# Four different row lengths for the tensors that the weight products stream from

## What is computed

```
swiglu(h):   (silu(h @ w_gate) * (h @ w_up)) @ w_down
conv_ffn(h): u = conv3(h @ w_up) + b;  (silu(u[:F]) * u[F:]) @ w_down
x = x + 0.5 * swiglu(norm(x)); x = x + token_mixing(norm(x))
x = x + cross_attention(norm(x), norm(mem)); x = x + 0.5 * swiglu(norm(x))
h = [meta; norm(x)]
for i in 0, 1: h = h + norm(mixer_i(norm(h))); h = h + norm(conv_ffn_i(norm(h)))
```

## Time and profile before

| | |
|---|---|
| median of 3 runs | 2238.99 us (2238.66 to 2241.04) |
| the profiled execution | span 2237.2 us from the first to the last instruction; 1.8 us less than the median of the runs |
| PE busy | 2184.0 us (98%), 14,619 products |
| DVE, ACT, POOL busy | 1354.7 us (61%), 999.2 us (45%), 960.0 us (43%) |
| mean granted clock of TensorE | 0.994 |
| DMA | 194.40 MB, mean 87 GB/s |

### The profile page before, as it was taken

One profiled execution on the slowest core, in us unless ns is written; L12 is line 12 of the kernel. 1 busy time (PEld: TensorE's weight loads), 2 busy tenths in 40 slices (PEclk: granted clock), 3 DMA queues, 4 the chain that ended last, 5 costly groups with the idle time before them and its releaser, 6 DMA issues.

```text
span 2237.2 us, 37596 instructions
## 1 busy us (share of the span) xinstructions
PE 2184.0 (98%) x14619; PEld 1971.6 (88%) x14619; DVE 1354.7 (61%) x2104; ACT 999.2 (45%) x1950; POOL 960.0 (43%) x709
## 2 busy tenths in 40 slices
PE   8999999999999999999999999999999979999998
PEld 6799998888887788989897779999999969989897
DVE  5785765637634557848577665762635797536255
ACT  4454453432443434636454446442423554424234
POOL 3644435642472455444451115244444503544443
PEclk9999999999999999999999999999999989999999
DMA  5243333331351223333310113133233301233331
GB/s 163 78 121 97 99 108 97 85 88 48 101 160 57 85 76 110 111 91 114 95 57 27 35 39 105 39 93 96 85 95 90 100 29 57 94 104 94 94 89 72
DMA packets 336251, 194.40 MB, mean 87 GB/s; under 512 B 7357, under 2 KB 327506, under 8 KB 336098
## 3 DMA queue, kind: packets, MB, share of 16 engines
q1 hardware_dynamic: 335570, 191.13, 29.2%
q10 hardware_dynamic: 528, 1.19, 0.2%
HBM read 190.20 MB, written 2.10 MB: 86 GB/s over the span
## 4 chain that ended last, share of the span: by engine, by line
PE 82%; DVE 11%; ACT 3%; issue 2%; POOL 1%; DVEq 0%; DMA 0%; POOLq 0%; ACTq 0%; SPq 0%
PE PS L830 17%; PE PS L834 17%; PE PS L832 17%; PE PS L1202 5%; PE PS L1203 5%; PE PS L1204 5%; PE PS L1125 2%; PE PS L1123 2%; PE PS L1124 2%; PE PS L3025 1%; PE PS L3008 1%; PE PS L3052 1%; PE PS L3070 1%; DVE u_conv L1651 1%; DVE mst L3258 1%
## 5 line engine op out<-in xcount | busy, mean ns | idle before, releaser
L754 POOL TENSOR_TENSOR w_lo<-raw,w_hi 128x512 fp32r<-128x512 f32 (+3 forms) x549 | 748.9, 1387 | 956.8 <-ACT w_hi L770 956.4
L770 ACT ACTIVATE w_hi<-raw 128x512 fp32r<-128x512 f32 (+3 forms) x549 | 305.0, 604 | 466.6 <-PE PS L834 362.5
L830 PE MATMUL PS<-XHI,w_hi 128*128 128x264 f32 (+2 forms) x1736 | 421.9, 308 | 4.1 <-DVE XLO L919 3.9
L834 PE MATMUL PS<-XHI,w_lo 128*128 128x264 f32 (+2 forms) x1736 | 413.2, 303 | 0.0
L832 PE MATMUL PS<-XLO,w_hi 128*128 128x264 f32 (+2 forms) x1736 | 413.0, 303 | 0.0
L830 PEld LDWEIGHTS PS<-XHI,w_hi 128*128 128x128 f32 x1736 | 280.0, 189 | 23.4 <-issue 6.5
L834 PEld LDWEIGHTS PS<-XHI,w_lo 128*128 128x128 f32 x1736 | 279.4, 189 | 13.4
L832 PEld LDWEIGHTS PS<-XLO,w_hi 128*128 128x128 f32 x1736 | 279.7, 189 | 13.1 <-issue 1.2
L830 PE MATMUL PS<-h_hi,w_hi 128*128 128x512 f32 (+2 forms) x588 | 180.1, 342 | 4.1 <-POOL w_lo L754 2.5
L832 PE MATMUL PS<-h_lo,w_hi 128*128 128x512 f32 (+2 forms) x588 | 179.5, 341 | 0.0
L834 PE MATMUL PS<-h_hi,w_lo 128*128 128x512 f32 (+2 forms) x588 | 179.5, 341 | 0.0
(11 more groups left out here) (567 smaller groups left out, 5420.9 us busy)
## 6 DMA issues: line engine op xcount, KB each, us to landing
raw<-in_ffn_w_up SPq DMA_DIRECT2D x132, 512.0 KB, 3.7
raw<-in_ffn_w_down SPq DMA_DIRECT2D x70, 512.0 KB, 3.7
raw<-in_ffn_w_gate SPq DMA_DIRECT2D x44, 512.0 KB, 3.7
raw<-in_w_in SPq DMA_DIRECT2D x25, 512.0 KB, 3.6
raw<-in_ffn_w_down SPq DMA_DIRECT2D x24, 384.0 KB, 3.4
raw<-in_xattn_w_kv SPq DMA_DIRECT2D x16, 512.0 KB, 3.8
raw<-in_w_out SPq DMA_DIRECT2D x8, 512.0 KB, 3.9
raw<-in_xattn_w_q SPq DMA_DIRECT2D x8, 512.0 KB, 3.9
```

The lines of the kernel that those rows point to most:

```text
L754: ins = nc.gpsimd.tensor_tensor(d, r, h.bitcast(F32), ALU.subtract)
L770: ins = nc.scalar.activation(d, r, ACT.Copy)
L830: nc.tensor.matmul(ps, wh, ahi(k)[:, c:c + w], start=(k == 0), stop=False)
L834: ins = nc.tensor.matmul(ps, wl, ahi(k)[:, c:c + w], start=False, stop=(k == u.kt - 1))
```

## The change

The rows of the four tensors get different lengths: XHI 560 elements (2240 bytes), XLO 568 (2272), h_hi 580 (2320), h_lo 536 (2144). All of them hold 528 elements. Filler tensors (`x_rest`, `h_line`, `h_rest`) take up the difference, so that everything behind stays in its place, and XLO and h_lo begin again at a multiple of 256 bytes (43264 and 161024). No instruction is added, removed or moved; only the addresses in the accesses to these four tensors differ.

```diff
 ROW = 576
+X_HI_ROW, X_LO_ROW, H_HI_ROW, H_LO_ROW = 560, 568, 580, 536
...
-    XHI = sb("XHI", [P, KD, ROW], F32R)
-    XLO = sb("XLO", [P, KD, ROW], F32R)
+    XHI = sb("XHI", [P, KD, X_HI_ROW], F32R)
+    XLO = sb("XLO", [P, KD, X_LO_ROW], F32R)
+    sb("x_rest", [P, KD * (2 * ROW - X_HI_ROW - X_LO_ROW)])
...
-    h_hi = sb("h_hi", [P, 8, ROW], F32R, ffn_scope)
-    h_lo = sb("h_lo", [P, 8, ROW], F32R, ffn_scope)
+    h_hi = sb("h_hi", [P, 8, H_HI_ROW], F32R, ffn_scope)
+    sb("h_line", [P, 32], scope=ffn_scope)
+    h_lo = sb("h_lo", [P, 8, H_LO_ROW], F32R, ffn_scope)
+    sb("h_rest", [P, 8 * (2 * ROW - H_HI_ROW - H_LO_ROW) - 32], scope=ffn_scope)
```

## The result

| | before | after |
|---|---|---|
| median of 3 runs each | 2238.99 us | 2256.08 us (2253.18 to 2258.59) |
| ratio | | 1.0074, 95% interval 1.0054 to 1.0094 |
| profiled execution | 2239.0 us, span 2237.2 | 2253.2 us, span 2251.4 |

The account below looks back on a forecast made before the run. PE's own pace, from one product's start to the next, was taken as the bound. The terms -1.5 - 0.6 - 0.4 + 1.1 - 1.5 = -2.9 us took 2239.0 to 2236.1 us; 8-in-10 range 2228 to 2247.

Parts of the forecast that it names:

- A: 512-column products streaming from h: 800 of 960 changed, -1.9 ns each, -1.5 us; bounds -2.7 and +5.3.
- B: 512-column products streaming from X: 328 of 984 changed, -0.6 us; bounds -1.1 and +2.2.
- C: Seven-product stage of ffn1: 192 of 576 products reading XHI and XLO rows changed, -0.4 us; bounds -0.6 and +1.3.
- D: 264-column products from X and h: 704 changed, losing 1.5 ns each, +1.1 us; bounds 0 and +4.7.
- E: 258-column products from X, 1920 of them: already at 12.0 ns extra, so 0; high bound +2.1 us.
- F: Row products of lines 1123 to 1125: 220 leave the slow 233.3 ns pace, -1.5 us; bounds -2.9 and 0.
- G: Weights operands from XLO (line 1882): 0; +0.6 us should its 96 products fall into the slow pace.
- rival 3: Slow state lasts in 512-column h products and 264-column halves, one step of 6.67 ns: +7.8 us, 2246.8; chance 0.24.
- rival 2: Nothing moves, only a product's length counts: 2239.0, or 2237.5 with F alone; chance 0.12.

Follow-up runs that it names:

- the table: Paces by offset from programs of zeros without the reference's work; 512 columns: 233.3 ns with weights blocks alone 8 elements past the mark, 226.7 with both.

## Why the prediction was wrong

So the sign of A and B was wrong: forecast -1.5 and -0.6, measured +4.6 and, with lines 2060 to 2062, +4.7. A is inside its high bound of 5.3. B is over its bound of 2.2, since a third of its products was counted as changed and the mean over all of them moved.
- **C, the seven-product stage:** right in sign, -0.4 forecast, -1.0 measured, below its low bound of -0.6; ffn2, whose tiles don't move, kept its 120.0.
- **D, 264 columns:** right in sign, +1.1 forecast, +5.9 measured, over its high bound of 4.7: 1.6 to 2.0 ns in the mean of all 3531 intervals, not 1.5 on 704.
- **E, 258 columns:** 0 forecast, +1.5 measured, inside its high bound of 2.1.
- **F, the row products:** -1.5 forecast, +0.1 measured. That the weights operand's offset held them slow was right, as h from element 60 shows with 2.7 us over its intervals; but the new rows brought it onto a 64-byte mark for two rows in eight, at 16 and 32 elements past the 256-byte mark, and with the weights operand there the table has slow paces (48.2 and 45.1 columns of extra).
- **G:** 0 forecast, +0.5 measured, near its bound. The 96 products are those of lines 1880 to 1882 together, 32 each, and not of line 1882 alone; XHI and XLO as weights operands moved against the streamed weights.
- **The rivals:** rival 3, the slow pace as the lasting one, came nearest: the right sign, and at 512 columns almost the size of its step (231.3 to 232.2 against 233.3). It had neither the 264-column pace (122 for 126) nor the extent, half of 2344 products, and it too was counted by 64-byte marks. Its counter-argument, 258-column products off the marks that never fell, carried one width's paces over to another width. In rival 2 stood the Trainium skill (SBUF - State Buffer, "Who interferes with whom"), by which TensorE's read ports leave it waiting on nobody: with no other engine at work the paces still are 226.7 to 233.3 ns by address. The section is about engines that get in each other's way, and none does here; the conclusion that no layout matters does not follow from it and is refuted by these paces.
- **Not foreseen:** the clock's fall at 396 us, 3.3 us in the profiled execution.

The range's upper end, 2247, stopped at a rival's middle. The sum of all high bounds, +16.2, is the result nearly to the microsecond, but by chance: B and D are above their high bounds, C is below its low one, and the fall of the clock was in none of them.

## What to carry to other kernels

Where PE is the bound and its stream is dense, start the streamed rows and the weights blocks that they meet at multiples of 256 bytes, and keep row lengths a multiple of that: for 512 columns no pair of offsets here was quicker. It isn't the best place for each width (256 columns gained at an offset of 28 elements). A pace measured at one width or offset is evidence for that width and offset alone: a table from a program of a few stretches of zeros gave the paces of this change to within a nanosecond. It didn't carry over to a stream that changes its offset from form to form, where it promised twice what came. And a gain of a microsecond or two must be read in the starts, since a fall of the clock worth 3 us comes and goes from kernel to kernel and from run to run.

## What the runs showed of the hardware

- In the two programs of zeros an fp32r product of 512 columns with its own weights block takes 226.7 ns at best and up to 235.6 (low rows 12 elements past the mark, high rows and weights on it) by the places of its two operands modulo 256 bytes. 256 columns take 113.3 to 120.1. Under 240 columns hardly anything more is saved: 128, 192 and 224 take 111.6 to 111.8 ns, 240 takes 112.1.
- The same addresses can hold two paces: 118.3 and 113.3 ns in one kernel, behind forms that read other places; 226.7 and 233.3 between two programs; and 226.7 and 233 for the row products behind their stop in kernels whose h rows stand alike.
- At the granted clock of 0.50 the extra is gone, in the changed kernel too: 0.426 us for 512 columns, as in the earlier trace rows.
- The Trainium skill (TensorE: Matmul & The Clock Gate, "Back-to-back issue gap") gives, for the gap of one product by itself, columns / 2.4 + 2.5 ns at full clock, 216 ns for 512, and columns / 1.2 at half, 427. The second agrees with the 0.426 us; for the first no address of these fp32r products came under 226.7. For a stream of weight loads and products it gives about 131 ns for 512 columns, without a type; the trace disagrees for fp32r, again 226.7.
